# The big products in one plain float32 pass instead of three split passes, with whole weight panels in eight slots and straight-line programs

## What is computed

```
for l in range(2):                                  # first block
    mod = silu(c) @ w_mod[l] + b_mod[l]             # 6 vectors of 1024: shift, scale, gate, twice
    p = (rms_norm(x, g1) * (1 + scale1) + shift1) @ w_in[l]
    mix = concat(attention, fourier, conv31, pool) @ w_out[l]
    x = x + gate1 * mix
    a, g = split((rms_norm(x, g2) * (1 + scale2) + shift2) @ w_ffn_in[l])
    x = x + gate2 * ((silu(a) * g) @ w_ffn_out[l])
# the same weights act on the context (256 tokens) in layer 0
# second block: an even layer (retention and short convolution), an odd layer (latent attention)
h = h + rms_norm(layer(rms_norm(h, pre)), post)
```

## Time and profile before

| | |
|---|---|
| median of 3 runs | 2432.48 us (2429.14 to 2433.07) |
| the profiled execution, first to last instruction | 2433.3 us |
| TensorE busy, matmul instructions | 2286.4 us (94%), 10994 |
| VectorE, ScalarE, GpSimd busy | 1196.1, 729.7, 747.4 us |
| moved by DMA | 213.33 MB, mean 88 GB/s |

### The profile page before, as it was taken

How to read it: one execution, slowest core, us unless ns; L and a number is a source line. 1 busy time by engine, 2 the same in 40 slices (tenths; PEclk the granted TensorE clock), 3 DMA queues, 4 the chain that set the end, 5 groups by cost and what they waited for, 6 DMA issues and landing times.

```text
span 2433.3 us, 29034 instructions
## 1 busy us (share of the span) xinstructions
PE 2286.4 (94%) x10994; PEld 1835.4 (75%) x10994; DVE 1196.1 (49%) x2168; ACT 729.7 (30%) x1053; POOL 747.4 (31%) x311
## 2 busy tenths in 40 slices
PE   5998888999999999798989999989999999899997
PEld 5885567888888888685678888877678888777655
DVE  6469957555545555478452212253432334521365
ACT  2322432322112221423442222233243222344442
POOL 3426002322322232330044444433214444333202
PEclk9998999999999999899999999999899999899898
DMA  7212223334333332121023322322112223221201
GB/s 256 72 58 78 87 70 104 101 124 134 111 102 121 129 132 84 66 66 57 1 69 99 111 85 95 112 74 95 61 52 87 95 95 98 75 66 55 75 1 52
DMA packets 69368, 213.33 MB, mean 88 GB/s; under 512 B 7696, under 2 KB 11408, under 8 KB 69008
## 3 DMA queue, kind: packets, MB, share of 16 engines
q1 hardware_dynamic: 47232, 168.64, 21.1%
q10 hardware_dynamic: 22032, 43.26, 5.3%
HBM read 209.77 MB, written 2.10 MB: 87 GB/s over the span
## 4 chain that ended last, share of the span: by engine, by line
PE 83%; DVE 10%; ACT 4%; issue 2%; DMA 1%; POOL 1%; DVEq 0%; ACTq 0%; SPq 0%
PE prod L520 71%; PE misc L543 2%; PE misc L618 2%; DVE raw L1407 1%; DVE operand_lo L1327 1%; PE misc L606 1%; PE misc L802 1%; PE misc L557 1%; DVE stat L1479 1%; PE prod L861 1%; PE misc L588 1%; ACT operand_hi L947 1%; PE prod L790 1%; PE prod L693 1%; DVE work L1358 1%
## 5 line engine op out<-in xcount | busy, mean ns | idle before, releaser
L489 POOL TENSOR_TENSOR wlo<-raw,whi 128x1024 fp32r<-128x1024 f32 (+3 forms) x284 | 705.2, 2484 | 1592.7 <-ACT whi L881 1592.7
L520 PE MATMUL prod<-operand_hi,whi 128*128 128x512 f32 (+1 forms) x2208 | 734.9, 373 | 33.7 <-DVE operand_lo L1345 14.1
L520 PE MATMUL prod<-operand_lo,whi 128*128 128x512 f32 (+1 forms) x2208 | 725.3, 369 | 0.0
L520 PE MATMUL prod<-operand_hi,wlo 128*128 128x512 f32 (+1 forms) x2208 | 721.5, 367 | 0.0
L881 ACT ACTIVATE whi<-raw 128x1024 fp32r<-128x1024 f32 (+3 forms) x284 | 293.5, 1034 | 748.6 <-PE prod L520 748.6
L520 PEld LDWEIGHTS prod<-operand_hi,whi 128*128 128x128 f32 x2208 | 380.5, 190 | 120.4 <-issue 26.0
L520 PEld LDWEIGHTS prod<-operand_hi,wlo 128*128 128x128 f32 x2208 | 382.0, 190 | 71.8
L520 PEld LDWEIGHTS prod<-operand_lo,whi 128*128 128x128 f32 x2208 | 381.6, 190 | 68.8 <-issue 2.6
L520 PE MATMUL prod<-hidden_lo,whi 128*128 128x512 f32 (+1 forms) x528 | 160.9, 359 | 0.0
L520 PE MATMUL prod<-hidden_hi,whi 128*128 128x512 f32 (+1 forms) x528 | 159.0, 355 | 0.0
L520 PE MATMUL prod<-hidden_hi,wlo 128*128 128x512 f32 (+1 forms) x528 | 158.8, 355 | 0.0
(11 more groups left out here) (243 smaller groups left out, 2490.6 us busy)
## 6 DMA issues: line engine op xcount, KB each, us to landing
raw<-in_w SPq DMA_DIRECT2D x224, 512.0 KB, 3.3
raw<-in_w SPq DMA_DIRECT2D x32, 704.0 KB, 4.0
raw<-in_wmod SPq DMA_DIRECT2D x32, 512.0 KB, 3.6
cosT<-in_wmod ACTq DMA_DIRECT2D x64, 256.0 KB, 2.8
sinT<-in_wmod ACTq DMA_DIRECT2D x64, 256.0 KB, 3.0
dft<-in_dftx ACTq DMA_DIRECT2D x8, 512.0 KB, 4.6
resid<-in_xt SPq DMA_DIRECT2D x1, 3072.0 KB, 15.1
raw<-in_w SPq DMA_DIRECT2D x12, 192.0 KB, 2.3
```

The costliest lines, as they stand in the source:

```text
L489: nc.gpsimd.tensor_tensor(wlo[b][:, 0:w], raw[slot][:, 0:w], whi[b][:, 0:w].bitcast(F32), ALU.subtract).then_inc(lo_ready, 1)
L520: mm = pe.matmul(G[b][:, t0:t0 + tn], w[b][:, k * P:(k + 1) * P], a[:, t0:t0 + tn], start=(k == 0 and q == 0), stop=(k == g.kc - 1 and q = ...
```

## The change

- The types float32r are gone. `whi`, `wlo`, `operand_lo`, `hidden_lo`, `mix_lo`, `latent_*_lo` and the instructions that fill them are gone. `big()` issues one plain float32 matmul per k and width, with the weights straight from the landed panel.
- The weights' ring has 8 slots; a slot is free once TensorE has finished its panel.
- `mod_step` counts two reductions of 1024 per column instead of four of 512; the reduction starts from the value in `par` and writes it back. The last 64 columns come as whole panels into two buffers of their own (`modw`).
- The loops are written out.

```diff
-                    for k in range(g.kc):
-                        ...
-                        for q, (w, a) in enumerate(((whi, xh(k)), (whi, xl(k)), (wlo, xh(k)))):
-                            for t0, tn in segs:
-                                mm = pe.matmul(G[b][:, t0:t0 + tn], w[b][:, k * P:(k + 1) * P], a[:, t0:t0 + tn],
-                                               start=(k == 0 and q == 0), stop=(k == g.kc - 1 and q == 2))
+                    for k in range(g.kc):
+                        if p == 0 and hidden is not None:
+                            freed(pe, GEMM[hidden].j0 + 2 * k + 1)
+                        elif p == 0:
+                            wait(pe, operand, ready + k + 1)
+                        for t0, tn in segs:
+                            mm = pe.matmul(G[b][:, t0:t0 + tn], w[:, k * P:(k + 1) * P], source(k)[:, t0:t0 + tn],
+                                           start=(k == 0), stop=(k == g.kc - 1))
...
-            for g in GEMMS:
-                def body(i, u, g=g):
-                    ...
-                    nc.gpsimd.tensor_tensor(wlo[b][:, 0:w], raw[slot][:, 0:w], whi[b][:, 0:w].bitcast(F32),
-                                            ALU.subtract).then_inc(lo_ready, 1)
-                each_panel(pool, g, body)
...
-                nc.scalar.activation(whi[j_static % 2][:, 0:w], raw[j_static % RAW][:, 0:w], ACT.Copy).then_inc(hi_ready, 1)
...
+            def norm_plain(sources, gain, Wt, dst):
+                r = invert(NX, Wt)
+                for c, src in enumerate(sources):
+                    nc.vector.scalar_tensor_tensor(dst[:, c, 0:NX], src, gain[:, c:c + 1], r, ALU.mult, ALU.mult).then_inc(operand, 1)
...
+            def modulate(k, w):
+                wait(dve, mod_step, mods_done(k - 1))
+                for s in range(2):
+                    col = par[:, PAR["mod0"][0] + 2 * k + s:PAR["mod0"][0] + 2 * k + s + 1]
+                    nc.vector.tensor_tensor_reduce((junk, w)[s][:, 0:DC * P], w[:, 0:DC * P], silu_c[:, 1024 * s:1024 * (s + 1)],
+                                                   1.0, col, ALU.mult, ALU.add, col).then_inc(mod_step, 1)
...
             def finish2(unit, h, q0, qn):
-                o = (M1, MM)[h % 2]
                 dve.wait_ge(pv_done, unit)
-                nc.vector.tensor_tensor(SG[:, h, :], o[:, 0:NX], SG[:, h, :], ALU.mult).then_inc(gated, 1)
-                low_operand(XL[:, h, 0:NX], SG[:, h, :], XH[:, h, 0:NX])
+                nc.vector.tensor_tensor(XO[:, h, 0:NX], (M1, MM)[h % 2][:, 0:NX], SG[:, h, :], ALU.mult).then_inc(operand, 1)
```

More of the change, by code:

```diff
@@ L40 @@
 EPS = 1e-6
-RAW = 4
+RING = 8
 SBUF_END = 229312
@@ L146, in wait, with tok, units1, head_ends @@
 def wait(eng, sem, value):
-    if isinstance(value, int) and value <= 0:
-        return
-    eng.wait_ge(sem, value)
+    if value > 0:
+        eng.wait_ge(sem, value)
+def tok(l):
+    return (NT, SEGS) if l == 0 else (NX, SEGS[:1])
+def units1(l):
+    out = [(h, 128 * b, 0, NT) for h in range(4) for b in range(4)]
+    if l == 0:
+        out += [(h, NX + 128 * b, NX, NC) for h in range(4) for b in range(2)]
+    return out
+def head_ends(units):
+    ends, start = {}, 0
+    for n, u in enumerate(units):
+        if n + 1 == len(units) or units[n + 1][0] != u[0]:
+            ends[n] = (u[0], units[start][1], u[1] + 128 - units[start][1])
+            start = n + 1
+    return ends
+units2 = [(h, 128 * b, 0, 128 * (b + 1)) for h in range(8) for b in range(4)]
+def mixer_steps(l):
+    segs = range(len(tok(l)[1]))
+    steps = ([("mean", 0, s) for s in segs] + [("square", 0, 0), ("sum", 0, 0)] + [("spread", 0, s) for s in segs]
+             + [("silu", 0, 0)] + [(kind, m, s) for kind in ("pointwise", "pool") for m in range(2) for s in segs])
+    return {4 + k: step for k, step in enumerate(steps)}
+def op_order(units, steps):
+    ends, order = head_ends(units), []
+    for i in range(len(units)):
+        if i - 1 in ends:
+            order.append(("end", i - 1))
+        if i in steps and steps[i][0] in ("pointwise", "pool"):
+            order.append(("step", i))
+    order.append(("end", len(units) - 1))
+    return {what: k for k, what in enumerate(order)}
+RET_AT = [(0, 0, 512), (1, 512, 384), (3, 896, 128), (2, 1024, 256)]
+def mix_ops(l):
+    return len(op_order(units1(l), mixer_steps(l)))
+OPS, _at = {}, 0
+for _name, _n in (("win0", 8), ("small0", 2), ("mix0", mix_ops(0)), ("fin00", 8), ("win1", 8), ("small1", 2), ("mix1", mix_ops(1)),
+                  ("fin10", 8), ("eqk", 8), ("eg", 8), ("econv", 8), ("oin", 8), ("latent", 5), ("attn", 8), ("end", 0)):
+    OPS[_name] = _at
+    _at += _n
 def build_program(nc, d):
@@ L589, in rotate, with attention @@
                 n["rope"] += 1
-            def attention(units, score, value, out, keys_tiles, steps={}, step=None, ahead=1):
+            def attention(units, ops, score, value, out, keys_tiles, steps={}, step=None, ahead=1):
                 ends = head_ends(units)
@@ L740, in mixer_step @@
                         if k:
-                            pe.wait_ge(operand_lo, n["op"] + order["step", products[k - 1]] + 1)
+                            pe.wait_ge(operand, OPS[f"mix{l}"] + order["step", products[k - 1]] + 1)
                         if kind == "pointwise":
@@ L983, in end @@
                 def end(i):
-                    if i in ends:
+                    if i in ends and finish is not None:
                         act.wait_ge(pv_done, base + i + 1)
```

714 lines of the change are left out of this document (237 added, 477 removed).

## The result

The changed kernel takes 2784.36 us, median of 4 runs (2782.38 to 2787.76), the kernel before 2430.81 us (4 runs, 2420.42 to 2433.07). The ratio is 1.1479, 95% interval [1.1444, 1.1514]: slower by 353 us. The forecast was 2790, range 2735 to 2850. The profiled execution has a span of 2781.0 us at a mean clock of 0.98.

A forecast was written before the change was run, and what follows sets the result against it. TensorE, busy 94% of the span, was taken as the bound. From 2433 us, plain products add 432 to its stream and savings outside it take off 72: 2793, rounded to 2790, range 2735 to 2850.

The forecast's parts named there:

- The deciding term: TensorE's stream of big products: plain products cost more than three split passes, 2209 us against 1777, 432 more.
- One plain pass at a split pass's price: Rival: each big product on TensorE streams its columns once, so the kernel takes 1175 us; chance 2%.
- The rule that I set against the rows: The skill's N / 2.4 + 2.5 ns between TensorE matmuls; taken at its word, a stream of 560 us.
- The weight loads that I gave 12%: Rival: weight loads show through in TensorE's mixed 512 and 256 steps, adding 48 us, 2840 us; chance 12%.
- The clock did not drop oftener: Judges the rival that entries and attentions leave another 80 us at 1.2 GHz, losing 40 us, 2830; chance 8%.
- The savings outside: Time saved outside TensorE's stream of big products, 72 us of 656; range none to 130.
- The start: Kernel start: eight modulation columns at 0.6 us less each, 5 us; the eight slots add nothing.
- my theory: TensorE's plain-product price makes the 432 us; savings outside come from low parts, row sums and nothing else.
- Layer 0's attention: Shorter modulation sums (9.6 us) and sixteen low parts gone (about 8), partly hidden by TensorE: 17 us saved.
- Layer 1's attention: Ten low parts there, 0.69 us each and some waited for, go: 9 us saved.
- Last attention: High and low part at each head's end go, 1.3 us for 8 heads: 10 us saved.
- Entries, small panels, the weights' copy: Panel entries after normalisations save 21 us, 28 small panels 5, the weights' copy ahead of the root 5.

The follow-up runs named there:

- Run 1: Kernel before with one plain float32 product per chunk on TensorE, all split parts still made: 2846.24 us, ratio 1.1721.
- run 7: Changed kernel's structure with three float32r products per chunk of one rounded weights copy by GpSimd, no low parts: 2367.79 us, ratio 0.9737.
- Run 5: Changed kernel with every 512-wide call of the big products issued as two of 256: 2798.46 us, ratio 1.1505.
- run 2: Kernel before with every low-part subtraction narrowed to 2 columns and three products of the high parts: 2386.71 us, ratio 0.9824.
- run 6: Changed kernel with 4 weight slots in place of 8: 2792.49 us, ratio 1.1481.
- run 12: Kernel before with whole-row sums, eight places at the start, and GpSimd's seven square additions there moved to VectorE: 2412.12 us, ratio 0.9929.
- run 3: Kernel before with whole-row modulation sums for rows passing through the weight slots: 2420.95 us, ratio 0.997.
- run 11: Changed kernel with every modulation row summed in two halves of 512 again: 2792.16 us, ratio 1.1479.
- run 10: Kernel before with whole-row sums and eight places instead of four for modulation rows at the start: 2413.06 us, ratio 0.9929.
- run 9: Kernel before with low-part subtractions 2 columns wide, three high-part products, and whole-row modulation sums: 2384.49 us, ratio 0.9811.

## Why the prediction was right, and where not

**The deciding term held.** A call of a big product is two records, 0.429 us each at 512 columns; a step of 768 is 1.2945 us where I had 1.29. Run 1 measures the term by itself, 420 us for 432, and run 7 takes 417 of it away again. The Trainium skill (FP8 and Floating Point Precision, TensorE Precision Notes) says that true float32 goes through the array four times; the runs agree: a step of 512 takes 0.858 us, 3.8 times the 0.226 of a float32r pass.

**The rivals.** One plain pass at a split pass's price is out by the counts and by the time of a record. The rule that I set against the rows, N / 2.4 + 2.5 ns (the Trainium skill, TensorE: Matmul & The Clock Gate, Back-to-back issue gap; the section gives it for an isolated matmul), fits the plain records if N is taken as 1024 for a record of a call of 512: 429.2 ns by the rule, 0.429 us in the rows. That such a record streams 1024 columns is worked back from this time; no view counts columns. Run 5's 2.3 ns for each added record is near the rule's constant. For a split pass the rule stays 10 ns short (216 against 226). The weight loads that I gave 12% are out by the 1.2945 us and by run 5. The clock did not drop oftener (0.98 against 0.961), and the stream is not held by the written-out code: TensorE shows no gap between records in the stretches above. No run writes out the loops alone; together with the waits for the high part they have what lies between runs 2 and 7, 19 us, less the row sums.

**The savings outside came to 84 us, 72 were forecast** (2433 - 1777 = 656 before, 2781 - 2209 = 572 after; 432 - 84 = 348 is the difference of the two profiled spans). By term:

- *The start*: forecast 5, measured 9.7. The step that failed is "the eight slots take nothing off by themselves there, VectorE is the slower side for most of it". With four slots, and with fewer rows ahead of `x`, the first product is 7.9 us later (run 6). VectorE was the slower side in part because rows were late (run 6), and because GpSimd kept it waiting (run 12). So my theory failed in its "nothing else": the places for landed rows were a third source.
- *Layer 0's attention*: forecast 17, measured 14.6, but made up of other things. "0.6 us less, 16 times, 9.6" failed: 0.5 us in the kernel before (run 3), 3.2 in the changed one (run 11). A unit's row sums did shrink by 0.5 us, and TensorE ended the unit instead, as the idle time of the next unit's reduction shows (VectorE's group in this stage, before and after: busy us, mean ns, idle before and releaser):

```profile
L1479 DVE TENSOR_REDUCE stat<-prod 128x1 f32<-128x768 f32 (+1 forms) x24 | 18.6, 773 | 1.7 <-PE prod L710 1.6
```

```profile
L1179 DVE TENSOR_REDUCE stat<-prod 128x1 f32<-128x768 f32 (+1 forms) x24 | 18.6, 775 | 12.9 <-PE prod L586 12.9
```

  The low parts, which I put at 8, gave 5 by their work (run 2); another 6, the remainder, I put down to the waiting for the high part, which no run shows alone.
- *Layer 1's attention*: forecast 9, measured 5.0. *Last attention*: forecast 10, measured 13.7, but 7.5 of these are the profiled execution of before itself, whose last attention took 93.1 us where runs 1, 3 and 10 have 83.8 to 85.7 with the same instructions. Against those the gain is 4 to 6.
- *Retention*: forecast nothing, measured 7.4, of which part is again such a difference (51.6 to 54.4 in kernels with low parts, 46.8 to 51.5 without them, 51.5 also in run 5).
- *Entries, small panels, the weights' copy*: forecast 21 + 5 + 5 = 31, measured 25 inside the panels and 8.5 at the five norms. The entry of `fin00` was to take 15.2 us from scaling to the end of the first panel; its 32 records are over at about 446.8, 15.2 us after 431.60, so this entry went as worked out.
- *The end* gave 0.8.

The forecast was near because the term of 432 was. The last 6 us are partly luck: the sum gave a span of 2793 and the profiled one is 2781, 12 less, which is what the savings exceeded 72 by; 7.5 of the 12 come from the one slow last attention of the execution that I started from, and rounding down to 2790 and a median 3 us above that span hide the other half. The small terms missed by 2 to 7 us each, two below (the attentions of layers 0 and 1) and three above (the start, the retention, the last attention).

## What to carry to other kernels

Count what TensorE must stream, not how many instructions it is given: a plain float32 product costs 3.8 float32r passes here, a split three; trading the split for the plain product frees every other engine and costs the one that is the bound a quarter more (2209 us of stream against 1777). Work taken from engines that lie beside the bound gives back only what its waits cost: 1458 us of busy time went for 62 to 84 us. Before an operation on the path is made shorter, ask which engine ends that unit next. And look at what runs beside a slow operation: at the start of the kernel before, whole rows gave 2.4 us, more places for them 2.1, and moving GpSimd's additions elsewhere 5.2.

## What was not expected of the hardware

**GpSimd stops VectorE.** While GpSimd adds tiles of 128x768, VectorE's reduction of 1024 with both inputs in SBUF takes 2.82 us instead of 1.22, and an addition of two columns 1.58 instead of 0.16 (run 10); without GpSimd's additions all are at their short times (run 12). An operation that starts in the gap between two additions keeps its 1.22 us. GpSimd's timeline beside the rows of run 10 above:

```profile
30.48 1.81 POOL L480 TENSOR_TENSOR work<-work,work 128x768 f32<-128x768 f32 x1 [0.95 <-ACT work L925]
33.25 1.86 POOL L480 TENSOR_TENSOR work<-work,work 128x768 f32<-128x768 f32 x1 [0.96 <-ACT work L925]
```

The first ends at 32.29, as VectorE's addition of two columns does (32.30); the second ends at 35.11, and the reduction 1.08 us later. The kernel before is full of this: VectorE's 21 additions of squares in `work` (line 1298) have a median of 2.47 us there and of 0.69 in run 2, where GpSimd's subtractions are narrow. Nearly all of it lay beside TensorE: TensorE waits 15.9 us for this line in both; ahead of `fin00`, for one, the last addition is made from 413.88 to 414.84 us, and GpSimd's next subtraction starts at 414.87. The Trainium skill (SBUF — State Buffer, "SBUF: two separate sides") calls the shared pair of ports an exclusive lock, held for a whole instruction, that a VectorE operation with two SBUF inputs needs too; the traces agree, down to the short operation that waits 1.4 us for its turn.

**Split passes have two rates.** A pair of a 512-wide and a 256-wide float32r pass takes 0.353 us in the kernel before and in runs 2, 3, 9 and 12 (567 to 569 records in 100 us), and 0.346 us in run 10, all at clock 1.00: 555.3 us instead of 565.7 from `fin00` to `fout01`. In run 7 the rate changes within one execution. The rows are 100 us in run 10, then in run 7 before and after the change (columns as above):

```profile
800.00:900.00 100.00, 100.00 (x579) 88.28 (x578) 58.19 (x129) 22.90 (x24) 31.34 (x12) 1.00 0.40 133
```

```profile
500.00:600.00 100.00, 100.00 (x578) 87.99 (x577) 33.49 (x51) 4.06 (x5) 13.78 (x12) 1.00 0.42 132
600.00:700.00 100.00, 100.00 (x569) 86.81 (x568) 35.66 (x58) 0.81 (x1) 11.70 (x9) 1.00 0.35 103
```

Plain pairs show one rate, 1.29 us a step, in every execution kept. What sets the rate of the split passes is open; it moves the price of the whole split stream by up to 15 us (720 steps), and so the term of 432.

**The same instructions, other times.** The kernel before lies between 2417.8 and 2439.2 us in 13 runs, the changed kernel within 5.4 us in 4. In the traces it is whole pauses that differ, the last attention (83.8 to 93.1 us) and the retention (51.6 to 54.4), and the stretch above. What sets them I have not tried to find out; a term of a few us read in such a stage from one profiled execution is worth little.
